# A hybrid attention and mixture-of-experts layer: one weight load is issued without waiting for a gather, and two score products change places

## The reference, cut to what matters

```python
s1 = jnp.einsum('bhqd,bhkd->bhqk', q1, k1, preferred_element_type=jnp.float32) * scale
s2 = jnp.einsum('bhqd,bhkd->bhqk', q2, k2, preferred_element_type=jnp.float32) * scale
a = jax.nn.softmax(s1, axis=-1) - lam * jax.nn.softmax(s2, axis=-1)
return jnp.einsum('bhqk,bhkd->bhqd', a.astype(v.dtype), v)
```

```python
def swiglu(t, wg, wu, wd):
    return (jax.nn.silu(t @ wg) * (t @ wu)) @ wd
```

## Time and profile before

| what | value |
|---|---|
| median of 3 runs | 1014.96 us (1013.5 to 1015.51) |
| the profiled execution | 1015.51 us |
| its span, first to last instruction | 1013.3 us |
| TensorE matmuls busy | 945.1 us, 93% of the span |
| VectorE, ScalarE, GpSimd busy | 519.9, 330.8, 396.8 us |
| mean granted TensorE clock | 0.98 |
| moved by the DMA engines | 298.04 MB, mean 294 GB/s |

### The profile page before, as it was taken

One profiled execution on the slowest core, in us unless ns is written; L12 is line 12 of the kernel. 1 busy time (PEld: TensorE's weight loads), 2 busy tenths in 40 slices (PEclk: granted clock), 3 DMA queues, 4 the chain that ended last, 5 costly groups with the idle time before them and its releaser, 6 DMA issues.

```text
span 1013.3 us, 13917 instructions
## 1 busy us (share of the span) xinstructions
PE 945.1 (93%) x4003; PEld 395.4 (39%) x4004; DVE 519.9 (51%) x697; ACT 330.8 (33%) x594; POOL 396.8 (39%) x299
## 2 busy tenths in 40 slices
PE   4899999999999999989999889996999999999696
PEld 1644444677456543323333223332333333333232
DVE  1347877786267835434554434443444454455246
ACT  4212221576245412313233232222223323322232
POOL 0313331000000156545565554555365665555430
PEclk9999999999999999989999999998999999999798
DMA  9955551450325959999989999999999999999946
GB/s 371 355 198 207 186 203 46 176 210 1 133 85 198 388 210 402 390 372 379 376 278 368 401 379 367 379 359 368 384 368 362 373 347 376 372 360 360 352 109 218
DMA packets 62669, 298.04 MB, mean 294 GB/s; under 512 B 14590, under 2 KB 15586, under 8 KB 34609
## 3 DMA queue, kind: packets, MB, share of 16 engines
q1 hardware_dynamic: 42850, 260.11, 64.7%
q0 software_dynamic: 18736, 35.41, 14.5%
q10 hardware_dynamic: 1056, 2.18, 0.6%
HBM read 282.15 MB, written 38.27 MB: 316 GB/s over the span
## 4 chain that ended last, share of the span: by engine, by line
PE 58%; DMA 33%; SPq 3%; DVE 3%; issue 1%; ACT 1%; ACTq 0%; DVEq 0%
DMA wring<-in_w_e_down 24%; PE psum L1251 17%; PE psum L1003 12%; PE psum L1263 7%; DMA wring<-in_w_e_up 6%; PE psum L1094 3%; PE psum L1074 3%; DMA heads<-in_w_ada 3%; PE psum L1065 2%; PE psum L1041 2%; PE psum L1213 2%; PE psum L979 2%; PE psum L1346 1%; SPq L475 1%; SPq L451 1%
## 5 line engine op out<-in xcount | busy, mean ns | idle before, releaser
L1251 PE MATMUL psum<-wring,xres 128*64 (+1 forms) x1664 | 378.5, 608 | 32.7 <-DVE wring L1705 32.6
L587 POOL DMA_INDIRECT xg<-h_rows,gidx x216 | 250.6, 1160 | 207.6 <-ACT gidx L840 129.3
L1251 PEld LDWEIGHTS psum<-wring,xres 128*64 128x64 f32 x1664 | 117.8, 140 | 255.1 <-issue 249.9
L1709 DVE STREAM_TRANSPOSE xres<-xg 128x1024 f32<-128x1024 f32 x53 | 108.4, 2045 | 175.4 <-DMA xg<-h_rows,gidx 172.9
L1263 PE MATMUL psum<-wring,rows 128*64 x416 | 187.0, 592 | 1.9 <-ACT rows L836 1.9
L1263 PE MATMUL psum<-rows 128*64 128x512 f32 x416 | 187.1, 592 | 0.0
L1705 DVE COPY wring<-wring 128x1536 f32 x106 | 126.2, 1232 | 42.4 <-SPq L464 41.4
L594 POOL DMA_INDIRECT expert_sums<-xres,sidx x50 | 87.3, 1746 | 91.3 <-DMA expert_sums<-xres,sidx 83.0
L898 ACT COPY xres<-psum 128x1024 f32<-128x1024 f32 x52 | 52.7, 1013 | 189.3 <-PE psum L1263 96.9
L1263 PEld LDWEIGHTS psum<-wring,rows 128*64 128x64 f32 x416 | 56.9, 137 | 120.1 <-issue 120.1
L836 ACT COPY rows<-wring 128x1024 f32 x104 | 103.5, 1046 | 0.3 <-SPq L468 0.3
(11 more groups left out here) (258 smaller groups left out, 866.5 us busy)
## 6 DMA issues: line engine op xcount, KB each, us to landing
wring<-in_w_e_gate SPq DMA_DIRECT2D x64, 1024.0 KB, 8.4
wring<-in_w_e_up SPq DMA_DIRECT2D x64, 1024.0 KB, 16.0
wring<-in_w_e_down SPq DMA_DIRECT2D x64, 1024.0 KB, 18.0
ring<-in_w_ada SPq DMA_DIRECT2D x20, 1024.0 KB, 4.8
ring<-in_w_in SPq DMA_DIRECT2D x3, 2048.0 KB, 26.0
heads<-in_w_ada SPq DMA_DIRECT2D x4, 1024.0 KB, 22.9
ring<-in_w_out SPq DMA_DIRECT2D x1, 4096.0 KB, 13.5
acc<-expert_sums SPq DMA_DIRECT2D x8, 512.0 KB, 7.4
```

Of the source, the lines that this page charges most:

```text
L587: pool.indirect_dma_start(xg[q][:, 256 * s:256 * s + 256], None, hrows, bass.IndirectOffsetOnAxis(gidx[:, q, s:s + 1].bitcast(U32), 0), bo ...
L1251: last = pe.matmul(pp[2][SUB * g:SUB * g + SUB, 512 * q:512 * q + 2 * F] .rearrange("p (u f) -> p u f", u=2), xT[:, q, k, SUB * g:SUB * g ...
L1709: dve.transpose(xT[:, q].rearrange("p k (s r) -> p s k r", s=4), xg[q].rearrange("p (s r k) -> p s k r", s=4, k=KD)).then_inc(s_xte, 1)
```

## The change

Two edits. SyncE no longer waits on `s_gt[0]` ahead of `load_gate_up(NB)`; the wait on `s_gu` stays. And `scores` issues its first two calls in the other order: (0, 0, 512) first, then (1, 0, 256). The third and the fourth call, the wait on `s_scs` and the signals stay with their calls.

```diff
             sp.wait_ge(s_sh_st[0], 16)
             load_down(NB)
             sp.wait_ge(s_gu, NT)
-            sp.wait_ge(s_gt[0], 64)
             load_gate_up(NB)
...
                 t, h = divmod(u, HEADS)
-                for s, c0, n in ((1, 0, 256), (0, 0, 512), (1, 256, 512), (0, 512, 256)):
+                for s, c0, n in ((0, 0, 512), (1, 0, 256), (1, 256, 512), (0, 512, 256)):
                     o0 = 2 * KEYS * (u % 2) + KEYS * s + c0
                     if (s, c0) == (0, 512):
                         pe.wait_ge(s_scs, u + 1)
```

## The result

The changed kernel takes 1021.07 us (median of 6 runs, 1016.97 to 1023.14), against 1014.23 us for the kernel before in the same series (6 runs, 1010.86 to 1015.77). The ratio is 1.006 with a 95% interval of 1.0042 to 1.0079, so it is slower by 4 to 8 us. The ratio isn't the quotient of these two medians, which would be 1.0067; 23 executions of the changed kernel are on record in all, and their median is 1019.87 us. The forecast of 1014.5 us was wrong, and 1021.07 lies above its range, which ended at 1020.0 (1019.87 would lie just inside it).

A forecast was written before the change was run, and what follows sets the result against it. Experts' passes were taken as bound in turns by TensorE and the weight stream, what precedes them by TensorE. Scores 0, lead -1.1, late gather +0.5, taken as -0.5 net: 1014.96 to 1014.5 us; range 1013.0 to 1020.0.

The forecast's parts named there:

- the one on the scores: Attention scores, 15 units on the chain: the new call order leaves each unit at 1.49 us, so 0 us.
- A: Score call (1, 0, 256), two matmuls on partitions 64 to 127; first in the old order, second in the new.
- B: Score call (0, 0, 512), two matmuls on partitions 0 to 63; second in the old order, first in the new.
- D: Fourth score call, (0, 512, 256), on partitions 0 to 63; waits for call (1, 0, 256), which writes the same bank.
- completion in order: Rival at every unit's scores: completion is signalled in program order, 0.35 x 15 = +5.2 us, 1019.7 us; 13 in 100.
- starts in order: Rival at the scores: matmuls start in program order, 0.42 x 15 = +6.3 us, 1020.8 us; 5 in 100.
- The gather: First block's gather, ahead of pass 0: sharing the engines with the early 2 MB makes it 0.5 us late (0 to 3.6).
- 0.2 us of cover: Ahead of pass 0: at most some 0.2 us of a late first transpose would be hidden.
- the gather late: Rival: first block's gather late by 2.5 us or more; at 3.6 us, +2.3 us net, 1017.3 us; 12 in 100.
- The lead: Weight stream: set 6's load leaves 7.9 us earlier, worth about 1.1 us (0.7 to 1.4), coming out at pass 6.

The follow-up runs named there:

- The half behind the second down product: Against the kernel before, old score order: set 6's gate weights (1 MB) wait for the second shared down product, up weights for the gather; ratio 1.0021.
- the load twice: Against the kernel before, old score order and gather wait kept: set 6's 2 MB also loaded once more, early, on another semaphore; ratio 1.002.
- the load alone: Against the kernel before: only the gather wait ahead of set 6's load is removed, score calls keep their old order; ratio 1.0003 (0.9991 to 1.0016).

## Why the prediction was wrong

**The step that failed** is the one on the scores: "If A passes B's second half as B passed A's, the unit still takes 1.49 us: 0 x 15 = 0." The condition held, the conclusion didn't follow. A passed B at the start, and its signal was held until B's second half, which stands ahead of it in the program, was done: D's weight load at 219.98 behind B's end at 219.9, `s_scs` up at 219.94. Two runs show that this is the whole of it: with D made to wait for B in the old order the loss is the same, and with B no longer than A it is gone. I had the right rival, "completion in order", at 5.2 us (0.35 x 15). Measured are 5.3 us in the profile (0.33 x 16) and 5.7 us in time. I gave it 13 in 100, because I let a row on starts speak for ends. I had written myself that for the ends the trace showed nothing, and then weighed the matter as if it did.

**The rule of the Trainium skill** ("TensorE: Matmul & The Clock Gate", "Part 3: Packing small matmuls — row/col tiling") has matmuls start and end in program order. For the signals of the ends the trace agrees (`s_scs` above); for the starts it doesn't: A's second half starts 0.2 us before B's, which stands ahead of it. The price that I had put on starts in order, 6.3 us or 0.42 in a unit, didn't come; a unit lost 0.33.

**The gather.** "The load is gone when the last piece lands: I take 0.5 us" was a wrong size. It was 2.9 us late in the changed kernel and 2.8 us alone, inside the bounds of 0 to 3.6. What was wrong in the reasoning is that the load had to be gone when the last piece lands; it has to be gone when the last piece is to start. The half behind the second down product shows that 1 MB is enough if it is under way then. I had also let the gather wait for single packets and not for the load; in that run not one of its packets was moved for 4.2 us. That pass 0 has at most 0.2 us of cover was wrong too: in all five runs with the gather late, pass 0 is late by 0.7 us less than the transpose (2.9 became 2.2 in the changed kernel). I had looked at when pass 0 began, and not at when its transpose would have let it: pass 0 starts 0.5 us behind the end of a late transpose, and before it was 1.2 us.

**The clock** was left out at pass 0. The 2.11 us of idle time ahead of it were followed by 3.3 us at the lower clock, and the pass took 1.7 us longer. So a gather late by 2.9 us made the load behind pass 0 late by 3.9. In the load twice, where the clock stayed up, 2.5 us made 1.7.

**The lead.** The load did leave 7.9 us earlier, and there was a hole in the stream ahead of the next load, though later than forecast. I priced the lead at 1.1 us. What the runs show is only the net: with the load alone, -0.9 to +1.6 us, although the next load is 3.8 us late. How much of that is the lead and how much was hidden in TensorE's idle time ahead of pass 6 is not settled. The load twice, which has the lateness and no lead, was 0.4 to 3.6 us slower, but its next load was only 1.7 us late, and its interval overlaps that of the load alone. So it doesn't part the two.

**The sum.** The two edits add up within their intervals: 1.0056 and 1.0003 against 1.006. The range ended at 1020.0 because it took each rival with the forecast's value for the other edit. With completion in order and the gather late at once, my own prices gave 1014.96 + 5.2 + 2.3 = 1022.5.

## What to carry to other kernels

Where matmuls of two row groups run at once and one call waits for another, put the call that is waited for ahead of longer ones in the program, whatever their row group. Behind a longer call it ran early here and was still reported late. A bulk load that is issued "for free" before a short gather is not free if it is under way when the gather's last piece is issued, and a few microseconds in either direction decided this here. When two edits are independent, the range has to take in both of their bad cases together.

## What the runs showed of the hardware

- A matmul can start before one that is ahead of it in the program, if that one is of the other row group and not ready (A's second half 219.1, B's 219.3). The semaphore of the one that passed rises only behind the other's end (219.94, with the ends at 219.49 and 219.90), and D's load went out at 219.98.
- With the 2 MB out at -10.6 a gather's first transpose came 5.9 us behind the last of its four issues in place of 3.0. With 1 MB it came on time when the load left at -10.6, and 3.2 us late when it left at -7.1. In the second case no packet of the gather's queue was moved for 4.2 us while the 1 MB passed, and its last piece landed 1.7 us behind that MB.
- The clock fell to 0.50 for 3.3 us behind 2.11 us of idle time of TensorE (2.00 in the load alone), and not behind 1.68 us in the load twice.
